# One core, two hybrid encoder layers: part of the next sub-layer's first tile is multiplied before the scale between sub-layers is known

## The reference

```python
x = x + 0.5 * rms_norm(swiglu(rms_norm(x, pre1), W_up, W_down), post1)
x = x + rms_norm(W_out [GLA | DiffAttn | Retention](rms_norm(x, pre2)), post2)
x = x + 0.5 * rms_norm(swiglu(rms_norm(x, pre3), W_up, W_down), post3)
```

## Time and profile before

| | us |
|---|---|
| median of 3 runs | 1365.39 (1364.96 to 1366.94) |
| the profiled execution | 1364.96 |
| its span, first to last instruction | 1363.2 |
| PE busy in the span | 1331.2 |
| DVE busy | 819.3 |
| ACT busy | 637.1 |
| POOL busy | 130.7 |

### The profile page before, as it was taken

The page is one execution under the profiler, slowest core; times in us unless marked ns, Lnnn a source line. Parts: engine busy times, 40 slices in busy tenths (PEclk is TensorE's granted clock), DMA queues, the critical chain, the costliest instruction groups (busy, mean ns, idle before and its releaser), DMA issues.

```text
span 1363.2 us, 24696 instructions
## 1 busy us (share of the span) xinstructions
PE 1331.2 (98%) x9613; PEld 1292.3 (95%) x9613; DVE 819.3 (60%) x1230; ACT 637.1 (47%) x1001; POOL 130.7 (10%) x131
## 2 busy tenths in 40 slices
PE   5999999999999999999999999999999999999998
PEld 5999999988889999999999999999888899999998
DVE  5755544687666855554485555448866678555542
ACT  5544433653456644434464443346435565444433
POOL 2000000361000300000030000004600020000000
PEclk9999999999999999999999999999999999999999
DMA  7555555543344455544544554455333345544552
GB/s 185 171 164 171 164 164 148 155 120 86 91 119 122 124 146 147 154 143 142 162 123 144 150 153 140 146 161 148 91 86 91 101 124 155 154 146 147 146 151 66
DMA packets 351753, 187.49 MB, mean 138 GB/s; under 512 B 6320, under 2 KB 348604, under 8 KB 351688
## 3 DMA queue, kind: packets, MB, share of 16 engines
q1 hardware_dynamic: 348368, 177.49, 45.8%
q0 software_dynamic: 2480, 8.10, 1.7%
q10 hardware_dynamic: 840, 0.99, 0.3%
HBM read 182.24 MB, written 4.33 MB: 137 GB/s over the span
## 4 chain that ended last, share of the span: by engine, by line
PE 92%; DVE 4%; DMA 1%; ACT 1%; issue 1%; DVEq 1%; ACTq 0%; POOL 0%; SPq 0%; POOLq 0%
PE ps L634 28%; PE ps L636 28%; PE ps L635 28%; DVE w_l L513 1%; DMA raw<-in_ffn_w_up_dram 1%; PE ps L930 1%; PE ps L829 1%; PE ps L804 1%; PE ps L943 1%; DMA par_in<-in_ret_norm_dram 0%; PE ps L902 0%; DVE probs L1478 0%; PE ps L687 0%; DVE z L1537 0%; DVE y L1320 0%
## 5 line engine op out<-in xcount | busy, mean ns | idle before, releaser
L634 PE MATMUL ps<-xn_l,w_h 128*128 128x320 f32 x1840 | 579.4, 315 | 4.0 <-DVE xn_l L1309 3.6
L636 PE MATMUL ps<-xn_h,w_h 128*128 128x320 f32 x1840 | 567.9, 309 | 0.0
L635 PE MATMUL ps<-xn_h,w_l 128*128 128x320 f32 x1840 | 567.8, 309 | 0.0
L513 DVE TENSOR_TENSOR w_l<-raw,w_h 128x1024 fp32r<-128x1024 f32 (+1 forms) x340 | 410.7, 1211 | 168.3 <-ACT w_h L504 168.1
L504 ACT ACTIVATE w_h<-raw 128x1024 fp32r<-128x1024 f32 (+1 forms) x342 | 353.4, 1035 | 235.2 <-DMA raw<-in_ffn_w_down_dram 129.1
L634 PEld LDWEIGHTS ps<-xn_l,w_h 128*128 128x128 f32 x1840 | 345.1, 188 | 14.6 <-DVE xn_l L1309 5.4
L635 PEld LDWEIGHTS ps<-xn_h,w_l 128*128 128x128 f32 x1840 | 345.3, 188 | 1.5
L636 PEld LDWEIGHTS ps<-xn_h,w_h 128*128 128x128 f32 x1840 | 345.1, 188 | 0.0
L634 PE MATMUL ps<-hid_l,w_h 128*128 128x320 f32 x704 | 217.3, 309 | 0.0
L635 PE MATMUL ps<-hid_h,w_l 128*128 128x320 f32 x704 | 217.3, 309 | 0.0
L636 PE MATMUL ps<-hid_h,w_h 128*128 128x320 f32 x704 | 217.3, 309 | 0.0
(11 more groups left out here) (242 smaller groups left out, 1118.3 us busy)
## 6 DMA issues: line engine op xcount, KB each, us to landing
raw<-in_ffn_w_up_dram SPq DMA_DIRECT2D x176, 512.0 KB, 3.8
raw<-in_ffn_w_down_dram SPq DMA_DIRECT2D x64, 448.0 KB, 3.8
raw<-in_w_in_dram SPq DMA_DIRECT2D x54, 512.0 KB, 3.8
raw<-in_ffn_w_down_dram SPq DMA_DIRECT2D x32, 512.0 KB, 4.0
raw<-in_w_out_dram SPq DMA_DIRECT2D x16, 512.0 KB, 4.0
const<-in_tables_dram POOLq DMA_DIRECT2D x8, 298.0 KB, 4.6
x_in<-in_x_prompt_dram SPq DMA_DIRECT2D x1, 1024.0 KB, 6.3
scores<-in_cache_diff_k_dram POOLq DMA_DIRECT2D x2, 512.0 KB, 5.4
```

The source lines that it names most:

```text
L513: dve.tensor_tensor(w_l[s][:, 0:cols], raw[s][:, 0:cols], w_h[s][:, 0:cols], ALU.subtract).then_inc(w_lo, 1)
L634: pe.matmul(out, w_h[s][:, w], xl, start=first, stop=False)
L635: pe.matmul(out, w_l[s][:, w], xh, start=False, stop=False)
L636: return pe.matmul(out, w_h[s][:, w], xh, start=False, stop=last)
```

## The change

At each of the five borders the first tile of the next sub-layer gets its first three blocks in two parts. One part is the product with the old x (times the pre gain) into bank 0, where the opening goes on with the blocks 3 to 7. The other is the product with y (times the same gain) into bank 4. DVE later multiplies bank 4 by the spread scale (`ahead_scale`) and adds bank 0 to it (`ahead_add`) before the first tile is read. The high and low parts of these six operands are made by ACT (`ahead_his`) and DVE (`ahead_los`), three of x and then three of y: in the down tiles of an FFN all six before `y_tile` and the add of tile 6, in the output tiles of the mixer three after tile 4 and three after tile 5. The opening leaves out three products of tile 0, and `keep_busy(6)` is `keep_busy(1)`. The first opening of the program has no part in it.

```diff
+AHEAD = 3
...
+            def ahead_part(l, u0, b, part, k0, k1):
+
+                if k0 == 0:
+                    pe.wait_ge(w_lo, l * UNITS + u0 + 1)
+                bank, at = (0, KD - AHEAD) if part == 0 else (4, KD - 2 * AHEAD)
+                for k in range(k0, k1):
+                    pe.wait_ge(ahead_lo, (2 * b + part) * AHEAD + k + 1)
+                    mm = product(ps[:, bank, 0:T], slot(l, u0), k, xn_h[:, at + k, :], xn_l[:, at + k, :], k == 0,
+                                 part == 1 and k == AHEAD - 1)
+                if part == 1 and k1 == AHEAD:
+                    mm.then_inc(ahead_used, 1)
+
+            def over_border(l, u0, ly, m):
+
+                b = ly * 3 + m
+                ahead_part(l, u0, b, 0, 0, 1)
+                spread(ly, m)
+                ahead_part(l, u0, b, 0, 1, AHEAD)
+                ahead_part(l, u0, b, 1, 0, AHEAD)
+                keep_busy(1)
+
+            def opening_step(l, u0, n, i, order=range(KD), xh=xn_h, xl=xn_l, done=0):
 
                 pe.wait_ge(xn_lo, (l * 4 + n) * KD + i + 1)
                 for t in range(OPENING):
+                    if t == 0 and i < done:
+                        continue
...
-                    opening_step(l, u0, n, i)
+                    opening_step(l, u0, n, i, done=AHEAD if l * 3 + m else 0)
...
                 opening(l, u0, n, m)
+                if l * 3 + m:
+                    pe.wait_ge(ahead_scaled, l * 3 + m)
                 up_pair(0, 2, False)
...
-                    spread(l, norm // 2)
-                    keep_busy(6)
+                    over_border(*((l, U_MIX) if norm == 0 else (l + 1, U_F1)), l, norm // 2)
...
                 opening(l, U_MIX, 1, 1)
+                pe.wait_ge(ahead_scaled, l * 3 + 1)
...
                 stat_y(l, 1)
-                spread(l, 1)
-                keep_busy(6)
+                over_border(l, U_F2, l, 1)
...
                 for k in range(KD):
                     act.wait_ge(x_new, (l * 3 + m) * KD + k + 1)
+                    if l * 3 + m and k == KD - 2 * AHEAD:
+                        act.wait_ge(ahead_used, l * 3 + m)
...
+            def ahead_his(l, norm, part, evicted):
+
+                if part:
+                    act.wait_ge(evac, evicted)
+                for k in range(AHEAD):
+                    src, at = (y, KD - 2 * AHEAD + k) if part else (x, KD - AHEAD + k)
+                    act.activation(xn_h[:, at, :], src[:, k, :], ACT.Copy, scale=gains[l][:, norm, k:k + 1]).then_inc(ahead_hi, 1)
...
+                if following:
+                    ahead_his(*following, 0, evicted)
+                    ahead_his(*following, 1, evicted)
                 y_tile(l, m, None, phase, 2, 0, norm + 1, SLOTS + l * UNITS + d0 + 3 * m + 3)
...
                     if v == N_OUT - 2:
                         hi(act, l, U_F2 + 3)
+                    if v in (N_OUT - 4, N_OUT - 3):
+                        ahead_his(l, 4, v - (N_OUT - 4), l * GROUPS + G_OUT + AHEAD)
...
                 post(l, n, norm, update)
+                if update:
+                    ahead_scale(l * 3 + m - 1)
                 sum_x(l, m)
...
+            def ahead_los(l, norm, part, b, evicted):
+
+                if part:
+                    dve.wait_ge(evac, evicted)
+                for k in range(AHEAD):
+                    src, at = (y, KD - 2 * AHEAD + k) if part else (x, KD - AHEAD + k)
+                    dve.wait_ge(ahead_hi, (2 * b + part) * AHEAD + k + 1)
+                    dve.scalar_tensor_tensor(xn_l[:, at, :], src[:, k, :], gains[l][:, norm, k:k + 1], xn_h[:, at, :],
+                                             ALU.mult, ALU.subtract).then_inc(ahead_lo, 1)
+
+            def ahead_scale(b):
+
+                dve.tensor_copy(sq[1][:, :], ps_rs[:, 0:T])
+                dve.drain()
+                dve.wait_ge(ahead_used, b + 1)
+                dve.tensor_tensor(sq[1][:, :], sq[1][:, :], ps[:, 4, 0:T], ALU.mult).then_inc(ahead_scaled, 1)
+
+            def ahead_add(rows):
+
+                dve.drain()
+                dve.tensor_tensor(sq[1][0:rows, :], sq[1][0:rows, :], ps[0:rows, 0, 0:T], ALU.add)
+                dve.drain()
...
+                    first = opened and isinstance(v, int) and v == 0
+                    if first:
+                        ahead_add(P)
...
+                if following:
+                    for part in range(2):
+                        ahead_los(*following, part, l * 3 + phase, l * GROUPS + g0 + KF + AHEAD)
                 add_square(l, m, phase, 0)
...
                     if v == 0:
-                        dve.tensor_tensor(alr[0:RANK, :], src[0:RANK, :], rs[0:RANK, :], ALU.mult).then_inc(evac, 1)
+                        ahead_add(RANK)
+                        dve.tensor_tensor(alr[0:RANK, :], sq[1][0:RANK, :], rs[0:RANK, :], ALU.mult).then_inc(evac, 1)
...
                     if v == N_OUT - 2:
                         lo(dve, l, U_F2 + 3)
+                    if v in (N_OUT - 4, N_OUT - 3):
+                        ahead_los(l, 4, v - (N_OUT - 4), l * 3 + 1, l * GROUPS + G_OUT + AHEAD)
```

More of the change, by code:

```diff
@@ L388, in build @@
         x_new = sem("x_new")
+        ahead_hi, ahead_lo = sem("parts_of_x_and_y_high"), sem("parts_of_x_and_y_low")
+        ahead_used, ahead_scaled = sem("parts_multiplied"), sem("part_of_y_scaled")
         y_norm = sem("y_norm")
@@ L644, in tile_part @@
                     mm.then_inc(w_used, 1)
-            def opening_step(l, u0, n, i, order=range(KD), xh=xn_h, xl=xn_l):
+            def ahead_part(l, u0, b, part, k0, k1):
[16 more added lines that the diff above has]
+            def opening_step(l, u0, n, i, order=range(KD), xh=xn_h, xl=xn_l, done=0):
                 pe.wait_ge(xn_lo, (l * 4 + n) * KD + i + 1)
                 for t in range(OPENING):
+                    if t == 0 and i < done:
+                        continue
                     if i == 0:
@@ L1109, in ffn @@
                     hi(act, l, d0 + 3 * m + t + 5)
+                following = None if last else (l, 2) if f == 0 else (l + 1, 0)
+                evicted = l * GROUPS + (G_F1 if f == 0 else G_F2) + KF + AHEAD
+                if following:
+                    ahead_his(*following, 0, evicted)
+                    ahead_his(*following, 1, evicted)
                 y_tile(l, m, None, phase, 2, 0, norm + 1, SLOTS + l * UNITS + d0 + 3 * m + 3)
@@ L1376, in ffn @@
                 f, phase = norm // 4, norm // 2
+                opened = l * 3 + phase > 0
                 def up_step(i, q, ahead, late):
@@ L1380, in up_step @@
                     dve.wait_ge(w_used, 6 * i + (SLOTS + l * UNITS + u0 + 2 * q + 2))
-                    dve.tensor_tensor(gate[q][:, :], ps[:, 2 * q, 0:T], rs[:, :], ALU.mult).then_inc(up_mul, 1)
+                    first = opened and isinstance(v, int) and v == 0
+                    if first:
+                        ahead_add(P)
+                    dve.tensor_tensor(gate[q][:, :], sq[1][:, :] if first else ps[:, 2 * q, 0:T], rs[:, :], ALU.mult).then_inc(up_mul, 1)
                     dve.tensor_tensor(up[q][:, :], ps[:, 2 * q + 1, 0:T], rs[:, :], ALU.mult).then_inc(evac, 1)
@@ L1422, in ffn @@
                     lo(dve, l, d0 + 3 * m + t + 5)
+                following = None if l == DEPTH - 1 and f == 1 else (l, 2) if f == 0 else (l + 1, 0)
+                if following:
+                    for part in range(2):
+                        ahead_los(*following, part, l * 3 + phase, l * GROUPS + g0 + KF + AHEAD)
                 add_square(l, m, phase, 0)
```

## The result

The changed kernel takes 1369.26 us as the median of 6 runs (1367.25 to 1373.21) beside 1366.76 of the kernel before in the same series; the measured ratio is 1.0027, with a 95% interval from 1.0015 to 1.0039 (the quotient of the two medians alone is 1.0018). The kernel before was predicted from a series with 1365.39; its median over all later series lay between 1366.3 and 1367.06. The profiled execution took 1367.25, its span 1365.5, where before had 1364.96 and 1363.2.

What follows compares the result with a forecast made beforehand. PE was taken as the bound, busy 98% of the span. Border terms +0.3, +2.6, -0.8, -0.8 and +2.1 gave +3.4 on 1364.96, so 1368.4, plus 0.4 for the median: 1368.8 us, range 1366.0 to 1371.0.

Steps and rivals of the forecast that it cites:

- the sum of +3.4: All five borders together: +0.3, +2.6, -0.8, -0.8 and +2.1 us, added to the profiled execution's 1364.96.
- the 0.4 that I added: Median of the runs taken as 0.4 us above the profiled execution, turning 1368.4 into 1368.8.
- The late `stat_y`: Mixer output tiles: splits delay DVE's last add, so PE's sums start 2.4 us late at border two, 2.8 at five.
- The price of 0.5 for a split: Mixer output tiles, DVE: each split takes 0.5 us with POOL idle, against 0.77 beside POOL's adds.
- An FFN border gains 0.8: Opening has three products fewer, 1.33 us; 0.54 is given back waiting for x's eighth low part.
- The idle for the eighth low part: In the opening, PE waits for x's last low part, ready at 455.85 whatever PE does; 0.54 us given back.
- The first border ends at +0.3: First layer's mixer: `ahead_add` and drains add 0.6 us, making `alr` late, so +0.3 instead of -0.8.
- The clock falls at both mixer borders: PE's clock drops after the sums: 1.0 us taken, +1.0 at border two, +0.1 at five, which had one already.
- the rival without the clock: Late `stat_y`, but no clock drop at either mixer border: +1.4, 1366.8 us; chance 0.20.
- Its cause: Mixer borders: PE idle 2.5 us and more, five times as long as where the clock dropped before, speaks for drops.

Runs made afterwards that it cites:

- two_ahead: The changed kernel with two blocks ahead instead of three and three filler matmuls instead of one; 1368.75 us, ratio to the kernel before 1.0009.
- ffn_only: The change at the three FFN borders alone, both mixer borders running the old code; 1366.61 us, ratio to the kernel before 0.9996.
- filler: The changed kernel with 5 and 7 filler matmuls in PE's wait for the last add at the mixer borders; 1368.85 us, ratio to before 1.0012.
- no_splits: The changed kernel without the six splits on ACT and DVE at the mixer borders, computing from other numbers; 1362.07 us, ratio to before 0.9976.
- early: The changed kernel with the mixer's splits behind output tiles 0 and 6 and a weight unit moved behind tile 6; 1366.91 us, ratio to before 1.0005.
- after_again: The changed kernel once more, without any edit, for more runs and a second profile; 1370.86 us, ratio to the kernel before 1.0032.
- early_2: Against `early`, ACT makes the high part of one weight unit of the next FFN ahead of tile 6; 1365.13 us, ratio to before 0.9987.
- unit_moved: The kernel before with only the third weight unit of the next FFN split after the last adds; 1366.54 us, ratio to before 0.9999.

## Why the prediction was right, point by point

The way, the size and the mechanism were right: 1368.8 forecast, 1369.26 measured, and the sum of +3.4 stands against +2.3 in the span and +2.5 between the medians. That the level came out within 0.5 us is partly luck. The sum was 1.1 too high for the profiled execution, and the median lay 2.0 above that execution instead of the 0.4 that I added; the two misses nearly cancel.

Border by border (the stretch, the wait for the last add and, at the first, the 0.63 behind it) the forecast was +0.3, +2.6, -0.8, -0.8 and +2.1, and the profile has -0.1, +2.1, -0.7, -0.7 and +2.0. The rest of the difference is the 0.31 by which the first border came sooner. Its steps:

- **The late `stat_y`** was the main term: 2.4 and 2.8 us, and it was shown three times over (with the change, without its splits, and the splits alone). The waits were 2.41, and 3.44 instead of 0.56, so 2.4 and 2.9. The price of 0.5 for a split held (1.47 for three).
- **An FFN border gains 0.8**: 0.71 to 0.74. The idle for the eighth low part was not 0.54 but 0.33. But the two starts around it were 0.63 and 0.26 apart, where running matmuls are 0.15 apart, so 0.59 was lost in all, about what I took. That the third block is worth nothing is the same term, seen from the other side in `two_ahead`; I had it in the sum and did not draw that conclusion.
- **The first border ends at +0.3**: mis-sized. It ended at -0.1 (-0.73 in the stretch, +0.63 behind it). `alr` was not late at all: from the sums' second half to its start it is 22.67, and it was 22.66. The reciprocal started 0.27 sooner in that measure, because `stat_x` and so ACT's root came sooner and it no longer waited for them; and in the lambda operations behind it a gap of 0.40 fell away. Both together cover `ahead_add`. PE did wait, but 0.42 instead of 1. The timeline of DVE there, against the earlier trace rows:

```profile
270.74 2.15 DVE L1399 RECIPROCAL rs<-sq 128x320 f32<-128x320 f32 x1
...
274.40 0.48 DVE L1436 TENSOR_TENSOR sq<-sq,ps 16x320 f32<-16x320 f32 x1 [0.32 <-issue]
274.95 0.48 DVE L1694 TENSOR_TENSOR ssum_x<-sq,rs 16x320 f32<-16x320 f32 x1
```

And PE's user of it, in PE's timeline:

```profile
275.48 0.80 PE L826 MATMUL ps<-ssum_x,a 16*128 16x320 f32 x2 [0.42 <-DVE ssum_x L1694]
```

- **The clock falls at both mixer borders**: it did, in both profiles of the changed kernel. The price was over-sized for the profiled execution: 17.25 - 16.79 = 0.46 and 17.54 - 16.79 = 0.75, where I took 1.0 each (at the fifth, 0.1 more than the 0.88 that it had). Over many runs it counts more than that. By the line above the change costs 1.4 to 1.7 at clock 1, near the +1.4 of the rival without the clock, and what is left of the difference between the medians, about 1.1 in the first series and 2.9 in the second, goes with the lower mean clock.
- **Its cause** was only argued, and half of it fell. I had taken the length of the idle for the cause. It is not what decides: at the mixer borders the clock fell after waits of 0.18 (`ffn_only`, second border) and 0.36 (`filler`), and it stayed up after 0.18 (`no_splits`, fifth), 0.74 (`ffn_only`, fifth) and 2.07 (`early`, fifth). But some wait does go with it. Of the 22 mixer borders of the eleven profiles PE waited in the sums (for the last add or for the last square) at 18, by 0.18 to 3.44, and at 15 of these the clock fell. At the other four, and at the 33 FFN borders, where any wait in the sums was 0.17 or less, it never fell. The Trainium skill's page "TensorE: Matmul & The Clock Gate" (section "What's actually happening") ties the clock to how busy the array has been. No run contradicts that, but these rows show that the length of one wait is a poor measure of it.

What stays open is what decides, after one and the same wait, whether the clock falls. Inside the first mixer PE waits 2.23 or 2.24 us for DVE near 312 us in all eleven profiles. Before had no fall there and `after_again` had one (at 313.61); PE's timelines of the two, before first:

```profile
312.11 0.70 PE L829 MATMUL ps<-sq 32*64 32x64 f32 x40 [2.24 <-DVE probs L1478]
...
313.11 0.77 PE L856 MATMUL ps<-sq 32*64 32x64 f32 x40 [2.23 <-DVE probs L1556]
```

The fall came in six of the eight profiles in which the first border is changed and in none of the three in which it is not. Its price is about 1.5 us (from `stat_x` to the next sums, without the wait for the last add, 174.55 in `after_again` and 173.01 in the first profile of the changed kernel). That may explain why `ffn_only` did not show its whole gain. The three without are too few to tell it from chance, and no experiment was made on it.

## What to carry to other kernels

Work that is moved ahead of a border lands on the engines that prepare the border: before it is moved, look not at their busy share (DVE 60%, ACT 47%) but at whether they have idle time between the target place and the last thing that the waiting engine needs from them. Where one of several parallel inputs paces the start (here the eighth low part of x), taking work off the bound engine pays only down to that pace, so a smaller dose gives the same gain. And a reordering that cures one wait should be read for the next one on the other engine before it is timed.

## What the runs showed of the hardware

- Six low parts of 128x320 on DVE, with POOL idle, took 1.47 for three, 0.49 each (the row of a single one is 0.55 long); beside POOL's adds the row of one is 0.77.
- In eleven profiles the granted clock fell at 15 of the 18 mixer borders at which PE waited 0.18 us or more in the sums, and at none of the 37 borders of either kind at which it waited 0.17 or less. How long the wait was did not tell: a fall followed 0.18 and 0.36, and none followed 0.74 and 2.07. This is a count and not a test; no run made PE wait at an FFN border.
- A fall of 3.4 us behind the sums cost 0.44 to 0.90 where products follow the spread (0.44 in `after_again`, 0.90 in `two_ahead`) and 0.88 to 1.08 where filler does. One of 6.8 us cost 1.9 to 2.5 (`early_2`, `two_ahead`, `unit_moved`).
